# Two attention layers with expert lookups, then a recurrent layer: row chunks reordered, weighted sums on the whole array

## The reference

```python
for l in range(2):
    qa, ka, va, qb, kb, vb = split(h @ w_in[l])            # 8+8 query heads of 64, 2+2 key and value heads
    oa = softmax(rope(norm(qa)) @ rope(norm(ka)).T / 8) @ va          # branch a: all 256 keys
    ob = softmax(qb @ kb.T / 8 - slope * dist, window 128, sink) @ vb # branch b
    mix = concat(rms_norm(oa), rms_norm(ob)) @ w_o[l]
    h = layer_norm(ALPHA * h + mix)
    q = h @ peer_wq[l]                                      # 8 heads x 2 halves x 128
    s = q @ sub_keys.T; top 16 of 128 in each half, top 16 of the 256 sums -> 16 experts a head
    a = gelu(u[expert] . h);  ffn = sum over the 128 experts of g * a * v[expert]
    h = layer_norm(ALPHA * h + ffn)
# then a layer with retention and delta-rule mixers (states from the context, then from h)
# and a mixture of 64 experts with 8 chosen for each token
```

## Time and profile before

| | |
|---|---|
| median of 3 runs | 2924.0 us (2923.17 to 2926.06) |
| the profiled execution | 2928.04 us, its span 2926.2 us |
| mean granted TensorE clock | 0.836 of full |
| PE busy | 2148.5 us, 73% of the span |
| DVE busy | 1582.8 us, 54% |
| ACT busy, POOL busy | 813.4 us, 843.2 us |
| moved by DMA | 891.48 MB, 305 GB/s over the span |

### The profile page before, as it was taken

The page is one execution under the profiler, slowest core; times in us unless marked ns, Lnnn a source line. Parts: engine busy times, 40 slices in busy tenths (PEclk is TensorE's granted clock), DMA queues, the critical chain, the costliest instruction groups (busy, mean ns, idle before and its releaser), DMA issues.

```text
span 2926.2 us, 33545 instructions
## 1 busy us (share of the span) xinstructions
PE 2148.5 (73%) x11740; PEld 1089.7 (37%) x11740; DVE 1582.8 (54%) x3254; ACT 813.4 (28%) x2292; POOL 843.2 (29%) x723
## 2 busy tenths in 40 slices
PE   6988677666766989676767666789878677667573
PEld 3657111121211559232323221568764532222221
DVE  4426857678544645888979865455552522121111
ACT  1402343433433212343343533322210111111110
POOL 1001444445432100454445553012110111222221
PEclk9889687677866989688888997899989788888887
DMA  7744999999999414999999999412112599999994
GB/s 282 263 169 159 421 422 422 420 412 395 422 422 378 194 37 160 381 421 375 413 378 403 422 421 417 159 42 74 58 62 101 210 404 401 388 391 381 382 379 146
DMA packets 130146, 891.48 MB, mean 305 GB/s; under 512 B 23216, under 2 KB 23600, under 8 KB 31792
## 3 DMA queue, kind: packets, MB, share of 16 engines
q0 software_dynamic: 86976, 553.74, 46.9%
q1 hardware_dynamic: 42992, 335.50, 28.6%
HBM read 880.21 MB, written 40.37 MB: 315 GB/s over the span
## 4 chain that ended last, share of the span: by engine, by line
PE 33%; DMA 33%; DVE 25%; ACT 4%; issue 4%; POOL 2%; SPq 1%; DVEq 0%; ACTq 0%; POOLq 0%
PE ps L155 31%; DMA ring<-in_peer_uv,idx_u 18%; DVE ring L1343 8%; DMA ring<-in_w_gu 6%; DVE arena L76 6%; DMA ring<-in_w_down 3%; ACT arena L125 3%; DMA arena<-in_w_gu 2%; PE ps L158 2%; DVE iu L113 2%; DVE arena L109 2%; DVE arena L1343 1%; DMA arena<-in_w_down 1%; DVE arena L97 1%; DMA arena<-in_peer_uv,idx_u 1%
## 5 line engine op out<-in xcount | busy, mean ns | idle before, releaser
L155 PE MATMUL ps<-ring,arena 64*64 64x512 f32 (+4 forms) x5248 | 1057.6, 764 | 475.2 <-ACT arena L125 348.0
L1343 DVE CUSTOM_DVE_ANT_0 ring<-ring,h 128x1024 f32<-128x1024 f32 x448 | 561.3, 1253 | 298.2 <-DMA ring<-in_peer_uv,idx_u 264.5
L2424 POOL DMA_INDIRECT ring<-in_peer_uv,idx_u x448 | 500.6, 1117 | 676.6 <-PE ps L155 517.4
L155 PEld LDWEIGHTS ps<-ring,arena 64*64 64x64 f32 (+3 forms) x5248 | 264.2, 158 | 1118.3 <-ACT arena L125 762.2
L155 PE MATMUL ps<-arena 128*128 128x128 f32 (+7 forms) x2760 | 471.4, 434 | 133.7 <-ACT arena L125 65.8
L125 ACT ACTIVATE arena<-arena 128x1 f32<-128x1 f32 (+3 forms) x1093 | 294.2, 269 | 812.8 <-DVE arena L1343 693.2
L155 PEld LDWEIGHTS ps<-arena 128*128 128x128 f32 (+4 forms) x2760 | 290.2, 191 | 325.4 <-ACT arena L125 150.7
L76 DVE TENSOR_TENSOR arena<-arena,ps 128x512 f32<-128x512 f32 (+1 forms) x158 | 93.6, 593 | 429.3 <-ACT arena L125 356.3
L155 PE MATMUL ps<-ring,hT 128*128 128x512 f32 (+2 forms) x896 | 310.2, 507 | 15.2 <-DVE hT L97 9.7
L125 ACT ACTIVATE arena<-ps 128x512 f32<-128x512 f32 (+5 forms) x192 | 106.4, 554 | 754.9 <-PE ps L155 707.5
L155 PEld LDWEIGHTS ps<-ring,hT 128*128 128x128 f32 x896 | 173.8, 200 | 140.9 <-issue 115.2
(11 more groups left out here) (116 smaller groups left out, 1394.6 us busy)
## 6 DMA issues: line engine op xcount, KB each, us to landing
ring<-in_w_gu SPq DMA_DIRECT2D x98, 1024.0 KB, 28.5
ring<-in_w_down SPq DMA_DIRECT2D x52, 1024.0 KB, 30.7
ring<-in_w_in SPq DMA_DIRECT2D x16, 2048.0 KB, 12.5
arena<-in_w_gu SPq DMA_DIRECT2D x30, 1024.0 KB, 29.9
ring<-in_w_mod SPq DMA_DIRECT2D x12, 2048.0 KB, 7.8
ring<-in_peer_wq SPq DMA_DIRECT2D x8, 2048.0 KB, 7.8
ring<-in_w_o SPq DMA_DIRECT2D x6, 2048.0 KB, 10.4
ring<-in_w_gates SPq DMA_DIRECT2D x12, 1024.0 KB, 4.9
```

Of the source, the lines that this page charges most:

```text
L155: return self.e.matmul(o, lhsT, rhs, start=start, stop=stop, skip_group_check=True)
L1343: v.done(v.e.tensor_tensor_reduce(out=row, in0=row, in1=h[:, n // 128, :], scale=1.0, scalar=0.0, op0=ALU.mult, op1=ALU.add, accum_out=aa[ ...
L2424: g.e.indirect_dma_start(out=landing(n), out_offset=None, in_=d["peer_uv"], in_offset=bass.IndirectOffsetOnAxis(ap=idx_u[:, n:n + 1], axis ...
```

## The change

What it does:

- **Order.** `attention` and the query part of `peer` are replaced by `first_chunk(l)` and `second_chunk(l)`. The first does keys and values for both chunks, but scores, powers, values, w_o, layer norm, queries and key scores for chunk 0 alone, and then the gathers begin. The second does the same for chunk 1 as the first part of the background, in the first 72 gathers. Layer 1's work for chunk 0 that needs only chunk 0 of h (`next_rows(1)`: transposes, three products with w_in, rope, transposes of keys and queries) is the last part of layer 0's background.
- **`beside`.** Two of three gathers below n = 72 carry a background step. After that every third in layer 0 (every second from 222 on), where it was every sixth, and every second in layer 1, where it was every third.
- **Attention inside.** Heads are paired (two key heads side by side in 128 columns), so one transpose serves two heads; the exponentials are scaled before their transpose; values are computed already transposed, and the norm's means and factors go over TensorE (`spread`, `spread_back`) in place of the transposes of the mix. Exponentials, maxima and scaling are done in two halves.
- **Weighted sums.** Two products of 128 columns in place of four of 64, and the diagonal is 128 x 128 where it was 128 x 64.
- **Loads.** The first 144 columns of the constants, which hold the identity and the powers of minus one half, are loaded ahead of the rest. w_mod comes in halves into two ring places of its own. peer_wq is loaded twice in each layer, once for each chunk (8 MB more a layer). w_in of layer 1 is loaded in layer 0's gathers. In layer 0, gathers 6 and 7 wait for the last block of w_mod to be used.

```diff
 def beside(l, n):
+    if n < 72:
+        return 1 if n >= 2 and n % 3 else 0
     if l:
-        return 1 if n in range(10, 250, 3) else 0
-    return 1 if n in range(10, 246, 6) else 0
+        return 1 if n < 250 and n % 2 == 0 else 0
+    return 1 if n in range(72, LAST_ROWS, 3) or n in range(LAST_ROWS, 252, 2) else 0
...
+            def first_chunk(l):
...
+                turned_rows(2 * l, 1)
+                run(project(l, 0, 1))
...
+                scores(l, 1, 0)
+                run(project(l, 1, 1))
...
+                scores(l, 0, 0, free)
                 modulation(0)
+                run(project(l, 2, 1, free))
+                turned_powers(l, 1, 0, free)
                 modulation(1)
+                values(l, 1, 0, free)
+                turned_powers(l, 0, 0, free)
+                spread(l, 1, 0, free)
                 modulation(2)
+                spread_back(l, 1, 0, free)
+                values(l, 0, 0, free)
+                spread(l, 0, 0, free)
+                spread_back(l, 0, 0, free)
+                run(out_rows(l, 0, free))
                 modulation(3)
...
+            def second_chunk(l):
+
+                yield
+                for br in (1, 0):
+                    scores(l, br, 1, OTHERS)
+                    yield from idle(3)
+                    turned_powers(l, br, 1, OTHERS)
+                    yield from idle(2)
+                    values(l, br, 1, OTHERS)
+                    yield
+                    spread(l, br, 1, OTHERS)
+                    yield
+                    spread_back(l, br, 1, OTHERS)
+                    yield from idle(2)
+                yield from out_rows(l, 1, OTHERS)
...
                     for x in range(2):
-                        for r in range(2):
-                            i, o = slice(64 * r, 64 * r + 64), slice(64 * (r ^ x), 64 * (r ^ x) + 64)
-                            t = pe.mm(two[x][o, :], diagonals[n % 2][i, :], landing(n)[i, D + 512 * x:D + 512 * x + 512],
-                                      k == 0, k == 127)
+                        t = pe.mm(two[x][:, :], diagonals[n % 2], landing(l, n)[:, D + 512 * x:D + 512 * x + 512],
+                                  k == 0, k == 127)
...
-                    peer(l, context_states())
+                    peer(l, chain(second_chunk(l), context_states()))
                 else:
-                    peer(l, chain(context_rows(), conv_features(ctx_side, hcT, ctx_side.conv_blocks, 0, OTHERS)))
+                    peer(l, chain(second_chunk(l), context_rows(),
+                                  conv_features(ctx_side, hcT, ctx_side.conv_blocks, 0, OTHERS), next_rows(1)))
...
-                    a.act(diagonals[n % 2], C("ident2"), ACT.Copy, ("diagonal", l, n), scale=w)
+                    a.act(diagonals[n % 2], ident, ACT.Copy, ("diagonal", l, n), scale=w)
...
+                    elif i >= 6 and l == 0:
+                        for half in range(2):
+                            g.wait_ge(*at("used", "w_mod", 11, half))
...
+                for i in range(4):
+                    block(Y_AT[l][i % 2], 4, d["peer_wq"][l, i], ("loaded", "wq", l, i, 1),
+                          after=[("used", "wq", l, i - 2, 1) if i > 1 else ("used", "w_o", l, i)])
```

More of the change, by code:

```diff
@@ L1278, in topk, with next_rows @@
+            def next_rows(l):
+                take_kt(hT, ("hT", 2 * l), 0, 0)
+                v.wait_ge(*at("features stored"))
+                yield
+                yield
+                take_rows(l, 0, 0)
+                yield
+                yield from rope(l, "k", 0)
+                yield
+                yield from rope(l, "q", 0)
+                yield
+                biases(0)
+                yield from idle(4)
             def topk(groups, n, vals, ids, src, alt):
@@ L2058, in peer @@
[L2058 to L2073 removed]
+                take_peer_queries(l, 3, 0)
@@ new lines, in next_rows @@
+            def next_rows(l):
+                take_kt(hT, ("hT", 2 * l), 0, 4)
+                a.wait_ge(*at("features stored"))
+                yield
+                yield from idle(3)
+                take_rows(l, 1, 0)
+                yield
+                yield
+                take_rows(l, 2, 0)
+                yield
+                take_keys(l, 1, 0)
+                take_queries(l, 1, 0)
+                yield from idle(3)
+                take_keys(l, 0, 0)
+                take_queries(l, 0, 0)
+                yield
@@ new lines, in sync_program @@
+                for i in range(2):
+                    block(Y_AT[l][i], 4, d["w_o"][l, i], ("loaded", "w_o", l, i), after=last)
+                into_p(d["peer_keys"][l], ("loaded", "keys", l), [("used", "w_in", l, 0)])
+                norm_rows(2 + 4 * l, "ln1", l, [("used", "ln2", 0) if l else ("used", "ln0", 0)])
+                if l == 0:
+                    modulate(1)
+                for i in range(2):
+                    block(X_AT[l][i], 4, d["peer_wq"][l, i], ("loaded", "wq", l, i, 0), after=[("used", "w_in", l, 1 + i)])
```

1128 lines of the change are left out of this document (623 added, 505 removed).

## The result

| | before | after |
|---|---|---|
| median of 4 runs | 2923.6 us | 3081.8 us (3076.9 to 3086.7) |
| span of the profiled execution | 2926.2 us | 3076.2 us |
| moved by DMA | 891.48 MB | 906.90 MB |

What follows compares the result with a forecast made beforehand. Transfers were taken to bound both gather stages, chained products and the work between them the attention stages. 2926.2 - 90 + (741 - 685) - 71 + (700 - 679) gave 2842 of span, forecast 2840 us, range 2790 to 2905.

Steps and rivals of the forecast that it cites:

- the middle: Layer 1 from layer 0's last sum up to its first gather: 139 us instead of 210, first gather at 1050.
- the first gather: Layer 0, work ahead of the gathers: first gather issued at 170 us for 259.7, 90 us earlier.
- the last layer: Behind layer 1's gathers: 1096 us, unchanged plus or minus 5, with the same loads and first waits.
- rival 4: Gather stages: TensorE at the lower clock makes it slower, 2999 us at 0.80, deciding at 0.85; chance 0.10 in all.
- both gather stages: Layer 0's gathers bound by transfers, 741 us; layer 1's, with TensorE level with the transfers, 700 us.
- steps on which TensorE waits: Layer 1's gathers: 35 us added for more background steps, closer together, on which TensorE waits.
- Rival 2: Background beside gathers: TensorE waits for norms or exponentials, sums behind it stop; 55 us more, 2895 us; chance 0.26.
- the sign that I named: First 72 gathers: long waits of PE behind DVE or GpSimd would show the forecast wrong.
- The whole-array edit: Weighted sums: priced at nothing in layer 0; in layer 1 120 us of TensorE time, 98 against a transfer bound.
- A cover of 125 us: Layer 0's gathers: TensorE's sum of 616 us under 741 us of transfers, spare time to hide the whole-array sums.
- w_mod's late blocks: Layer 0's start of gathers: PE starts late behind the last modulation blocks, at no cost if it catches up.
- block 11's use: Layer 0, last modulation block, needed before the seventh gather: placed at 190 to 205 us.

## Why the prediction was wrong

**Right, or near:** the middle, 139 forecast and 144 measured (1031 to 1174.7); the first gather, 170 forecast and 185 measured; the last layer, 1096 and 1094. The granted clock is 0.87 to 0.96 in the gathers, over the 0.85 at which rival 4 decides, so that rival is out. These stages hold an error of 15 + 5 - 2 = 18 us.

**Wrong: both gather stages.** Layer 0's took 846 us (185 to 1031) where I had 741, layer 1's 807 (1175 to 1982) where I had 700. With the 18 us, 105 and 107 make the whole miss: by its edges the forecast ends at 170 + 741 + 139 + 700 + 1096 = 2846, and 2846 + 230 = 3076. (The prediction's own sum gives 2842: it ends layer 1's gathers of before at 1834 and starts the last layer at 1830, 4 us counted twice.)

The step that failed is the cost of the waits of the background: nothing in layer 0, where I only asked whether TensorE's sum of work was below the transfers', and "I add 35 us for steps on which TensorE waits" in layer 1. TensorE's busy time was not the error: in the 244 us above it did 189 us of work, and the transfers that ran in them fill 0.78 of the time, 190 us. The 55 us of idle time are the loss there. Rival 2 came nearest ("the sums behind it stop"), but at a multiple of the 55 us that I gave it and not by its path. It had TensorE itself wait for a norm or for exponentials. In the traces of both stretches beside the attention (231 to 475 and 1175 to 1450 us) TensorE finds these ready and waits for diagonals alone, since VectorE and ScalarE are in their own attention steps. So the sign that I named, long waits of TensorE behind VectorE or GpSimd in the first 72 gathers, did not show, and the loss was there all the same. The two stages miss by 212 us, of which w_mod, the whole-array edit and the context, below, have their parts. I took the price from the context's steps, on which TensorE waited 10.4 us in layer 1; those are short and stand at every third gather. The attention's steps stand at two gathers in three, the long ones take 6.8 us on VectorE and 8.2 us on ScalarE, and these hold up the dots and diagonals as well. With 29 of the 47 steps out of the loop the gathers fell by 100 and 68 us.

**The stop is a loss of lead, in part.** That it matters at which gather VectorE's and ScalarE's steps stand was shown by moving them alone: 31 us. It was not all; with the shift 6 to 80 still take 243 us where the absence of 29 of the 47 steps gives 210 and the kernel before 191. What bounds it then I could not settle: the runs with seven places disagree between the layers.

**The whole-array edit: cover misjudged.** I priced it at nothing in layer 0 and 98 to 120 us of TensorE time in layer 1. It costs 53 us, about the same in each layer (27 and 23), and nothing in the kernel before. A cover of 125 us over a whole stage was an average: beside the attention TensorE's work and its waits lie end to end, and there the edit costs 20 of the 27 us and all of the 23. The groups of TensorE in layer 1, 1175 to 1982 us, give 516 us for 256 sums, 2.02 each and not the 1.78 of the upper clock that I took:

```profile
L155 PE MATMUL ps<-ring,arena 128*128 128x512 f32 x768 | 389.1, 642 | 99.2 <-ACT arena L125 99.1
L155 PE MATMUL ps<-arena 128*128 128x512 f32 x256 | 127.0, 622 | 54.6 <-ACT arena L125 54.6
```

**w_mod's late blocks: "no cost of its own if it catches up".** It doesn't catch up: without four of the blocks the kernel is 34 us faster. My explanation, argued and not tried by itself, is that TensorE can make good a late start only where it has time to spare against the transfers; beside the attention it has none (189 us of work and 55 us of waits in 244). I had placed block 11's use at 190 to 205 (it ended at 223), and priced the delay at nothing.

**Steps of the context packed closer: not priced.** Layer 0's gathers 128 to 192 took 47 us more than before, and a wider pace gave 28 back over the kernel. Of the load of the stored features only the bytes were in the sum, not the wait for them (11 us).

The account of the 158 us by runs: 53 quarter products, 7 more diagonals, 31 later steps, 17.5 the context's pace and features together, measured one on top of the other, are 109; w_mod's 34 was measured by itself, on the changed kernel, with work left out. If it adds, 15 us stay unassigned. That it adds wasn't tried.

## What to carry to other kernels

Work that is moved beside a pipeline costs more than its sum on the busiest engine. Look on every engine that the pipeline needs for steps longer than its lead (here 6.8 and 8.2 us against a gather every 2.6 us), and price each as a stop; that the length of the steps sets the price is my reading of the timelines, and no run changed it. Give the consumer's step a later place in its program than the producer's, by a few turns, and only where it measures well: the same shift gained beside the attention and lost beside the context. A cover is read in the stretch where the edit meets the new work, not over the stage.

## What the runs showed that I had not expected

Whole-array sums in the kernel before raise the mean granted clock from 0.836 to 0.917 and change the time by nothing; in the changed kernel quarter products lower it from 0.896 to 0.826 and are 53 us faster. In these four kernels the clock went with TensorE's busy time (2148 and 2378 us; 2379 and 2129 us) and said nothing of the kernel's time. One sum is 3.78 us at the lower level in the timeline above (four records, 252.47), and about 1.98 at the upper, as layer 1's end shows (granted clock 1.00 from 1965 to 1981 us). The period is 2.48 us there; the transfers were at 1.01 of their engines from 1930 to 1962 us:

```profile
1974.94 1.98 PE L155 MATMUL ps<-ring,arena 128*128 128x512 f32 x4 [0.51 <-ACT arena L125]
1977.42 1.98 PE L155 MATMUL ps<-ring,arena 128*128 128x512 f32 x4 [0.50 <-ACT arena L125]
```
